# Seven products for half of the contraction in two column chunks of the output projection

## The reference, cut to what matters

```python
merged = jax.nn.sigmoid(ga) * (o_a @ w_br_fox[l]) + jax.nn.sigmoid(gb) * (o_b @ w_br_dil[l])
x = x + merged @ w_out[l]            # (256 x 2048) @ (2048 x 2048)
h = rms_norm(x, g_ffn[l])
u = h @ w_up[l]                      # the feed-forward block begins
```

## Time and profile before

| | us |
|---|---|
| median of three runs (1336.2 to 1337.53) | 1336.95 |
| the profiled execution, whole | 1336.57 |
| its span in the trace | 1334.6 |
| PE busy | 1329.1 |
| DVE busy | 1122.2 |
| ACT busy | 940.6 |
| POOL busy | 156.2 |

### The profile page before, as it was taken

The page is one execution under the profiler, slowest core; times in us unless marked ns, Lnnn a source line. Parts: engine busy times, 40 slices in busy tenths (PEclk is TensorE's granted clock), DMA queues, the critical chain, the costliest instruction groups (busy, mean ns, idle before and its releaser), DMA issues.

```text
span 1334.6 us, 16448 instructions
## 1 busy us (share of the span) xinstructions
PE 1329.1 (100%) x6055; PEld 1101.9 (83%) x6055; DVE 1122.2 (84%) x1333; ACT 940.6 (70%) x1180; POOL 156.2 (12%) x175
## 2 busy tenths in 40 slices
PE   9999999999999999999999999999999999999999
PEld 7888888888888888888888888888888888888887
DVE  6768787888878876657789898999999999999996
ACT  6666666666666654446777778888888888888872
POOL 0121212021011000001010101111111102020200
PEclk9999999999999999999999999999999999999999
DMA  9877685758888655567879798999999999999952
GB/s 355 285 171 261 142 257 122 246 149 231 233 214 231 210 175 172 209 227 226 270 177 332 158 306 169 312 221 283 246 254 266 229 288 215 299 210 313 199 198 101
DMA packets 118175, 305.73 MB, mean 229 GB/s; under 512 B 11848, under 2 KB 13136, under 8 KB 117584
## 3 DMA queue, kind: packets, MB, share of 16 engines
q1 hardware_dynamic: 92288, 234.57, 50.4%
q0 software_dynamic: 21728, 66.07, 27.9%
q10 hardware_dynamic: 4080, 4.05, 0.9%
HBM read 302.55 MB, written 2.11 MB: 228 GB/s over the span
## 4 chain that ended last, share of the span: by engine, by line
PE 98%; DMA 1%; DVE 1%; ACT 0%; issue 0%; SPq 0%; ACTq 0%
PE acc L743 14%; PE acc L747 14%; PE acc L745 13%; PE acc L783 9%; PE acc L787 9%; PE acc L785 9%; PE acc L964 4%; PE acc L968 4%; PE acc L966 4%; PE acc L939 3%; PE acc L941 3%; PE acc L943 3%; PE acc L1076 1%; PE acc L768 1%; PE acc L766 1%; PE acc L764 1%
## 5 line engine op out<-in xcount | busy, mean ns | idle before, releaser
L1764 DVE TENSOR_TENSOR w_lo<-raw,w_hi 128x1024 fp32r<-128x1024 f32 x234 | 284.0, 1221 | 89.6 <-ACT w_hi L1250 88.4
L1250 ACT ACTIVATE w_hi<-raw 128x1024 fp32r<-128x1024 f32 x234 | 244.8, 1055 | 109.5 <-PE acc L747 75.9
L743 PE MATMUL acc<-w_hi,actA 128*128 128x512 f32 x664 | 261.7, 394 | 0.4 <-DVE w_lo L1764 0.3
L747 PE MATMUL acc<-w_hi,actA 128*128 128x512 f32 x664 | 259.1, 390 | 0.0
L745 PE MATMUL acc<-w_lo,actA 128*128 128x512 f32 x664 | 258.7, 390 | 0.0
L1250 ACT ACTIVATE w_hi<-raw_y 128x1024 fp32r<-128x1024 f32 x144 | 149.6, 1058 | 74.9 <-PE acc L747 22.4
L1764 DVE TENSOR_TENSOR w_lo<-raw_y,w_hi 128x1024 fp32r<-128x1024 f32 x144 | 173.2, 1220 | 23.1 <-ACT w_hi L1250 21.7
L1764 DVE TENSOR_TENSOR w_lo<-raw_x,w_hi 128x1024 fp32r<-128x1024 f32 x108 | 130.0, 1221 | 41.1 <-ACT w_hi L1250 40.9
L743 PEld LDWEIGHTS acc<-w_hi,actA 128*128 128x128 f32 x664 | 124.8, 188 | 26.3 <-issue 1.4
L747 PEld LDWEIGHTS acc<-w_hi,actA 128*128 128x128 f32 x664 | 124.7, 188 | 26.3
L745 PEld LDWEIGHTS acc<-w_lo,actA 128*128 128x128 f32 x664 | 124.8, 188 | 25.0
(11 more groups left out here) (296 smaller groups left out, 2598.8 us busy)
## 6 DMA issues: line engine op xcount, KB each, us to landing
raw<-w_in SPq DMA_DIRECT2D x102, 512.0 KB, 4.8
raw<-w_down SPq DMA_DIRECT2D x59, 512.0 KB, 5.7
raw_x<-w_up SPq DMA_DIRECT2D x44, 512.0 KB, 5.0
raw_y<-w_up POOLq DMA_DIRECT2D x34, 512.0 KB, 7.3
raw_x<-w_in SPq DMA_DIRECT2D x28, 512.0 KB, 4.3
raw<-w_out SPq DMA_DIRECT2D x28, 512.0 KB, 4.5
odd<-w_up SPq DMA_DIRECT2D x27, 512.0 KB, 5.2
work<-w_up SPq DMA_DIRECT2D x24, 512.0 KB, 5.4
```

The lines of the kernel that those rows point to most:

```text
L743: nc.tensor.matmul(o, lhsT=a_h, rhs=w_hi[:, s, k, :], start=first and k == 0, stop=False, skip_group_check=onto_seed)
L747: mm = nc.tensor.matmul(o, lhsT=a_l, rhs=w_hi[:, s, k, :], start=False, stop=last and k == KU - 1, skip_group_check=onto_seed)
L1250: nc.scalar.activation(w_hi[:, n % RING, :, :], src.rearrange("p (k n) -> p k n", k=KU), ACT.Copy).then_inc(hi_done, 1)
L1764: nc.vector.tensor_tensor(w_lo[:, n % RING, :, :], src.rearrange("p (k n) -> p k n", k=KU), w_hi[:, n % RING, :, :].bitcast(f32), ALU.subt ...
```

## The change

The output projection's 24 plain units become 30. Chunks 0 and 1 are taken as a pair (number 7, `PAIRS`): row tiles 0 to 7 by seven products in two quads, row tiles 8 to 15 plainly; chunk 2 stays plain and comes last. The units are numbered here from the first of the stage:

| unit | what | PE matmuls each |
|---|---|---|
| 0, 1 | P3 | 6 |
| 2, 3 | P1, then the last transposes of `tmp` | 6 |
| 4, 5 | P7 | 6 |
| 6, 7 | P6 | 6 |
| 8 | plain, chunk 0, j = 0 | 12 |
| 9, 10 | P5 | 6 |
| 11, 12 | plain, chunk 0 j = 1; chunk 1 j = 0 | 12 |
| 13, 14 | P2 | 6 |
| 15 | plain, chunk 0 | 12 |
| 16, 17 | P4 | 6 |
| 18 to 21 | plain, chunk 0, then chunk 1 three times | 12 |
| 22 to 29 | chunk 2 | 12 |

The token side needs four combinations of merged's quarters in a rounded and a rest part: ACT copies the transposed chunks 0 and 1 a second time into `odd` (four copies), DVE forms four differences (`make_merged`), ACT rounds them (`merged_part_high`) and negates a quarter for P1 (two copies), DVE writes the rests (`merged_part_low`). All this stands in the branch stage. The copies of P1's and P6's bank go to banks 1 and 3, so that the plain units of chunk 0 add onto them. The core of the diff:

```diff
+    units = product("P3") + product("P1") + product("P7") + product("P6") + plain(0, 0)
+    units += product("P5") + plain(0, 1) + plain(1, 0) + product("P2") + plain(0, 2)
+    units += product("P4") + plain(0, 3) + plain(1, 1, 2, 3)
+    return units + [("C", u) for u in range(UPR)]
...
-OUT_BANKS = ((6, 7), (1, 3), (0, 2))
+OUT_BANKS = {"P3": 6, "P1": 0, "P7": 7, "P6": 0, "P5": 0, "P2": 1, "P4": 3}
...   # PE, before the first quad of a product; and in a plain unit
+                    if name == "P3":
+                        pe.wait_ge(o_lo, NHEADS)
+                        pe.wait_ge(h_part_lo, 8)
+                    elif name == "P1":
+                        pe.wait_ge(dil_merged, 4)
+                        pe.wait_ge(h_part_hi, 12)
+                    elif name == "P7":
+                        pe.wait_ge(g_c22, PAIRS)
+                    elif name == "P6":
+                        pe.wait_ge(g_p1, PAIRS + 1)
+                    elif name == "P5":
+                        pe.wait_ge(g_v, PAIRS + 1)
...
+                for r, o in enumerate((bank[6], bank[0]) if side else (bank[1], bank[3])):
+                    if r and j == 0:
+                        pe.wait_ge(g_u0 if side else g_v, PAIRS + 1)
...   # ACT, branch stage
+                    if c < 2:
+                        nc.scalar.activation(merged_turned(c)[:, 2 * b:2 * b + 2, :],
+                                             bank[4 + b][:, :].rearrange("p (j s) -> p j s", j=2), ACT.Copy)
...
+                    elif c == 3 and u == 0:
+                        merged_part_high("P5", 9)      # then P7, P6, P3
+                    elif c == 3 and u == 1:
+                        act.wait_ge(mt_lo, 2)          # then two negated copies
...   # ACT, output stage
+            for n, unit in enumerate(OUTS, OUT_UNIT):
+                if unit in (("H", PAIRS, "P1", QU - 1), ("H", PAIRS, "P6", QU - 1)):
+                    out_sum(n, unit[2])                # waits for the unit, copies bank 0 to 1 or 3
+                high(n + RING)
+                if unit == ("H", PAIRS, "P3", QU - 1):
+                    act.wait_ge(merged, 4)
+                    act.dma_start(xr[:, :, :], x_rows).then_inc(x_again, 16)
+                elif unit == ("H", PAIRS, "P1", QU - 1):
+                    merged_high(3)
...   # DVE, branch stage
+                        if c == 2:
+                            make_merged()
                         dil_part(c)
...
+                    elif c == 3 and u == 1:
+                        merged_part_low("P5", 7)       # then P7, P6, P3
...   # DVE, output stage
+                if unit == ("H", PAIRS, "P5", QU - 1):
+                    dve.wait_ge(x_again, 16)
+                    dve.wait_ge(used, n + 1)
+                    add_bank(0, out_rows(0, 1)).then_inc(g_u0, 1)
...   # POOL
+            third_sum(PAIRS, 0)
+            third_sum(PAIRS, 1)
+            first_sum(PAIRS, 0)
+            first_sum(PAIRS, 1)
```

More of the change, by code:

```diff
@@ L110, with out_units, product, plain @@
 OUT_UNIT = BR_UNIT + 4 * UPR
-FF_UNIT = OUT_UNIT + 3 * UPR
+def out_units():
+    def product(name):
+        return [("H", PAIRS, name, q) for q in range(QU)]
+    def plain(side, *js):
+        return [("G", PAIRS, side, j) for j in js]
+    units = product("P3") + product("P1") + product("P7") + product("P6") + plain(0, 0)
+    units += product("P5") + plain(0, 1) + plain(1, 0) + product("P2") + plain(0, 2)
+    units += product("P4") + plain(0, 3) + plain(1, 1, 2, 3)
+    return units + [("C", u) for u in range(UPR)]
+OUTS = out_units()
+OUT_LOADS = [unit for unit in OUTS if unit[0] != "H"]
+OUT_LOAD_AT = {unit: k for k, unit in enumerate(OUT_LOADS)}
+OUT_AT = {unit: OUT_UNIT + n for n, unit in enumerate(OUTS)}
+FF_UNIT = OUT_UNIT + len(OUTS)
 GATE_PARTS = ("P3", "P5", "P6")
@@ L1554, in _ @@
                         merged_high(c - 1)
[L1556 to L1572, removed]
+                    elif c == 3 and u == 0:
+                        merged_part_high("P5", 9)
+                        merged_part_high("P7", 10)
+                        merged_part_high("P6", 11)
+                        merged_part_high("P3", 12)
+                    elif c == 3 and u == 1:
+                        act.wait_ge(mt_lo, 2)
+                        for half in range(2):
+                            nc.scalar.activation(own[:, 0, :, half * P:half * P + P],
+                                                 gate_quarter(0, 0, half).bitcast(f32), ACT.Copy, scale=-1.0)\
+                                .then_inc(h_part_hi, 1)
@@ L2140, in add_x2, with out_rows @@
                 t.then_inc(x2_done, 1)
[L2142 to L2148, removed]
-                    if u == 3 and c == 0:
-                        merged_low(3)
-                    elif u == 3 and c == 2:
-                        make_sums()
-                    elif u == 5 and c == 2:
-                        part_low("P3")
-                        part_low("P1")
-                    elif u == 6 and c == 2:
-                        part_low("P7")
-                        part_low("P6")
+            def out_rows(r, side):
+                return xr[:, r, side * NB:side * NB + NB]
@@ new lines, in _ @@
+            for n, unit in enumerate(OUTS, OUT_UNIT):
+                out_bank_sums(n, unit)
+                low(n + RING)
+                if unit == ("H", PAIRS, "P7", 0):
+                    merged_low(3)
+                elif unit == ("C", 3):
+                    make_sums()
+                elif unit == ("C", 5):
+                    part_low("P3")
+                    part_low("P1")
+                elif unit == ("C", 6):
+                    part_low("P7")
+                    part_low("P6")
```

214 lines of the change are left out of this document (174 added, 40 removed).

## The result

The changed kernel takes 1347.1 us (median of six runs, 1346.11 to 1348.42), the kernel before in the same job 1336.72 (six runs, 1336.2 to 1337.53). The ratio is 1.0078, with a 95% interval of 1.0067 to 1.0089: slower by 10.4 us, where 6.8 were forecast. The profiled execution took 1348.42 us, the longest of the six; its span is 1346.4, that of before 1334.6.

What follows compares the result with a forecast made beforehand. PE was taken as the bound, busy 1329.1 of 1334.6 us. -2.72 + 2.1 + 7.1 + 0.3 = +6.8 us on 1336.57 gave 1343.4, plus 0.4 for the median: 1343.8 us, 8-in-10 range 1338.0 to 1347.5.

Steps and rivals of the forecast that it cites:

- The removed matmuls: Output projection, chunks 0 and 1: 180 matmuls instead of 192, worth -2.72 us.
- Step 1: Stage start: DVE reaches `dil_part(3)` late, so PE waits before P1; +2.1 us, bounds 0 to 3.5.
- the walk: DVE's instructions before P1 added up in order from old-trace durations, putting the end of `dil_part(3)` at 558.4.
- the rival that DVE keeps pace: Added DVE work fits its gaps, no wait at P1, 1.75 us in unit 8; 1336.0 us; chance 0.12.
- Step 2: Middle of unit 8: PE waits for P6's bank copy, behind P5's high and its accumulating transfer; +7.1 us.
- the landing R: Landing of POOL's accumulating transfer for P5, q = 1: started at 562.6, 9.7 us long, so 572.3.
- x harmless: Rival: x's read does not slow the accumulating transfer, unit 8 waits 3.2 to 3.6 us; 1339.8 us; chance 0.22.
- Step 3: Unit 12's second half waits for DVE to empty bank 0 of P5; +0.3 us, from 0 to 1.5.
- The clock: Rival: clock falls while PE waits, nine matmuls at half clock cost 2.2 us; 1346.0 us; chance 0.24.
- Costs put at nothing: SP's reordered loads, later transposes and chunk 2 cost zero; up to 2.7 us per late unit if cover were gone.
- Asked for 8 us ahead: Data of SP's loads, transposes and chunk 2 is requested over 8 us early, covered by the ring of six units.
- the forecast's own: Main case, 1343.8 us with range 1341.5 to 1346.5 (unit 8's wait from 5 to 9.9); chance 0.42.

Runs made afterwards that it cites:

- The cured versions: Changed kernel with P6's copy first, early bank-0 sum, x's read split and feed-forward loads last: 1336.71 us; also x's second megabyte later, 1337.22; also late DVE rests, 1336.16.
- The best version measured: The kernel with feed-forward loads last and x's second megabyte later, plus DVE's rests for P5, P7, P6 behind `dil_part(3)`: 1336.16 us, ratio 0.9996.
- the late rests alone: Changed kernel with only DVE's rests for P7, P6 and P5 moved behind `dil_part(3)`: 1346.99 us, ratio 1.0075.
- x in pieces: Changed kernel with P6's copy first, bank-0 sum early, and x read in four pieces, 1.75 MB of it behind unit 7: 1340.4 us, ratio 1.0025.
- x's read later: Changed kernel with only ACT's 2 MB read of x moved from behind unit 1 to behind unit 7: 1342.11 us, ratio 1.0042.
- the copy first: Changed kernel with ACT's copy of P6's bank put before the highs of units 10 to 12: 1346.68 us, ratio 1.0079.
- the three cures with the late rests and loads: Kernel with copy first, early bank sum and x in pieces, plus DVE's rests behind `dil_part(3)` and SP's four early loads put off: 1340.54 us, ratio 1.0026.
- the bank sum early: Kernel with P6's copy first, plus DVE's sum of bank 0 moved ahead of the low of unit 13: 1344.0 us, ratio 1.0053.

## Why the prediction was right, and where it was not

**The removed matmuls.** Twelve fewer, in every profile after, and their -2.72 us. The cured versions show what is left of it: -2.7, with 1.5 us of waits of PE in the last profile, makes -1.2, and the medians give -0.7 with an interval from -1.7 to +0.7. The best version measured is thus not told from the kernel before.

**Step 1** held. `dil_part(3)` ends at 559.1 and P1 begins at 559.19, where 558.4 and 558.5 were forecast; 1.4 us of that are lost before the stage, so DVE was 0.7 us quicker than the walk. Its start-to-start cost is 1.7 us for 2.1. DVE had no idle time at all, as the walk said, and the rival that DVE keeps pace fell. What the prediction did not see is that this wait is worth nothing by itself: as unit 8 waits for a transfer that also hangs on DVE, it only moves there (the late rests alone). With every later wait cured, the same edit brought 1.06 us.

**Step 2** held in its place, its releaser and its size: 8.2 us for 7.1. Its terms, less the 1.4 lost before: the landing R at 573.1 for 572.3, as the transfer took 11.4 us, not 9.7 (the upper end was 12.5), while it started at 561.7 for 562.6; PE there 0.5 sooner; the copy 3.5 behind R for 3.65. That x slows it is shown by x's read moved away (6.1 us), and again by x in pieces (6.3), so the rival "x harmless" fell. The 512 KB even landed behind x's 2 MB, which took 9.5 us from an issue 0.26 us earlier. By the Trainium skill (DMA: Bandwidth & Descriptors, "Queues, rings and completion order") the engines take turns packet by packet between queues; the trace agrees, with 62 packets of x and 58 of POOL's in the same 2 us. While both ran, the shares went by packets, of which x has no more than the transfer, though four times the bytes. How many of the profile's packets make one turn is not seen, and the cause of the late first packet is not either. In the trace of before, x itself took 10.7 us, so the load of 559.1 did land with it, as the prediction said without a row for it.

**Step 3** did not appear: no wait at unit 12, for 0.3. It came up at 2.9 us once the copy was moved, from the chain that the step describes.

**The clock.** This is the step that failed. The sum put nothing for it, and the rival that held it had 0.24 of the chance against 0.42. Behind the wait of 8.0 us PE ran twelve slow matmul intervals, the first of 0.59 us and the others of 0.43, before it was back at 0.23: 2.5 us, for the rival's 2.2. That the two are close is partly luck: the earlier trace rows give 4.21 us for nine matmuls with the long end of the last one, from start to start they are 0.43 us apart and not 0.47, and the other waits brought 6 to 14 slow intervals, not nine. With the rival's price the forecast was 1346.0, and 1347.1 was measured. The evidence weighed against it was that the trace of before never shows a wait inside the kernel; that is absence, not evidence. The Trainium skill (TensorE: Matmul & The Clock Gate, "HAM oscillation — how this bites in real kernels") describes just this, a wait for a transfer that puts PE to half clock for the work behind it, and the trace agrees.

**Costs put at nothing.** SP's reordered loads cost nothing in the changed kernel, where its profile has no wait at chunk 2. They cost 3.7 us once the long wait was gone. The likely reason is that the long wait gave the loads the time that they lacked without it; no run shows this by itself. "Asked for 8 us ahead" was argued from the loads' own times and left out what SP's loads stand behind. And the 1.4 us lost before the stage were in no term. Such gaps are in some profiles with the early loads and not in others, and their cause is open.

**The sum.** On 1343.4 for the profiled execution come 2.5 (clock), 1.1 (step 2), -0.4 (step 1), -0.3 (step 3) and 1.4 (before the stage): 1347.7, of its 1348.42. The median of the runs is 1.3 lower than that execution, where the prediction added 0.4. The time lies within the range, 0.4 us below its upper end, next to the clock's case (1346.0) and not to the forecast's own (1343.8). The forecast's own range is also a little off by its own terms: step 2 from 5 to 9.9 gives 1341.7 to 1346.6, not 1341.5 to 1346.5.

## What to carry to other kernels

Fewer matmuls are worth their time only if every handover that they add is early: write down the waits in their order and ask of each what it turns into when it is cured. Here twelve matmuls fewer, worth 2.7 us, came out as a net loss of 10 us. Four edits together (the copy, the bank sum, x's read, SP's order) came out even; whether each of the four is needed was not tested. Where one late landing is behind several waits, moving an instruction off the first of them only names the next. A forecast with a wait of several us on a full PE should carry the slow matmuls behind it in its sum, not as a rival.

## What the runs showed of the hardware

- After a wait of PE of 8.0 us the granted clock was 0.50 and twelve intervals between matmuls of 128x512 were slow, 0.43 us instead of 0.23. Other waits and the slow intervals behind them: 2.8 us and 8 (x's read later), 2.9 and 7, 5.5 and 6 (the copy first), 2.9 and 8 (the three cures with the late rests and loads), 4.1 and 11 (the bank sum early), 8.2 and 14 (the late rests alone). So the clock fell behind waits of 2.8 us too, and the length of the slow stretch does not simply follow that of the wait. It costs 1.4 to 3.0 us a time; a wait of 2.9 us thus costs half as much again. After the waits of 1.6 us at P1 and of 1.8 at chunk 2 the clock stayed full.
- POOL's accumulating transfer of 512 KB took 6.1 to 6.4 us beside SP's loads, and 11.3 to 12.7 where the 2 MB read of x was issued within half a us of it. Cutting that read into four pieces and moving 1.75 MB of it brought 6.3 back; the pieces also go in packets of 2 and 4 KB instead of 8, and the runs do not separate that from the move.
- Two transfers of the same number of packets, 272, on two queues shared the time by packets and not by bytes: 62 packets and 0.51 MB of the one, 58 and 0.12 MB of the other, in the same 2 us.
